# Expert stage of a two-block model: all-token expert chunks spread singly among the row experts, mean sums inside the output projection, one register load ahead of the first routed weight load

## The reference, cut to what matters

```python
h = layer_norm_2(DEEPNORM_ALPHA * h + mixer(h), ...)   # y_out, layer_norm(2l)
y = hier_moe(h, ...)                                   # router, order, experts
h = layer_norm_2(DEEPNORM_ALPHA * h + y, ...)          # layer_norm(2l + 1)

def hier_moe(x, ...):        # 4 groups of 4 experts, hidden width 512
    g_idx = top-1 group of each token; e_w = softmax over its top-2 experts * g_w
    h = silu(x @ w_gate) * (x @ w_up) * gate_of_the_expert
    return h @ w_down
```

## Time and profile before

| | |
|---|---|
| median of three runs | 2466.53 us |
| the profiled execution | 2459.22 us, its span 2457.3 us |
| PE / DVE / ACT busy over the span | 92% / 62% / 43% |
| mean granted TensorE clock | 0.952 of 2.4 GHz |
| expert stage, layer 0: first chunk's matmul to the end of the last scatter | 1459.7 to 1831.6 us |
| expert stage, layer 1 | 2070.5 to 2436.6 us |
| of these, from gate of row expert 4 on | 233.8 and 230.6 us |
| weights read in such a stretch | 324 and 320 GB/s |

### The profile page before, as it was taken

How to read it: one execution, slowest core, us unless ns; L and a number is a source line. 1 busy time by engine, 2 the same in 40 slices (tenths; PEclk the granted TensorE clock), 3 DMA queues, 4 the chain that set the end, 5 groups by cost and what they waited for, 6 DMA issues and landing times.

```text
span 2457.3 us, 36662 instructions
## 1 busy us (share of the span) xinstructions
PE 2271.4 (92%) x13900; PEld 1894.5 (77%) x13900; DVE 1512.9 (62%) x2349; ACT 1068.1 (43%) x1514; POOL 234.8 (10%) x225
## 2 busy tenths in 40 slices
PE   7999999999999999899999679999989786999997
PEld 6677567999767756799976469987778476998875
DVE  3846365755384636575534565589985166658997
ACT  1142433343114244234433234467764264447775
POOL 1814000101181400011000000000000000000000
PEclk9999889999999989999999689999999998999999
DMA  4332113455333212356533125589964412458995
GB/s 164 124 118 79 52 61 129 163 181 173 119 125 124 70 52 69 131 176 195 185 125 107 43 80 170 192 294 349 346 248 165 144 44 102 157 197 318 353 348 188
DMA packets 109807, 396.86 MB, mean 161 GB/s; under 512 B 12088, under 2 KB 14144, under 8 KB 109376
## 3 DMA queue, kind: packets, MB, share of 16 engines
q1 hardware_dynamic: 108576, 393.45, 46.2%
q10 hardware_dynamic: 1056, 1.06, 0.2%
HBM read 393.40 MB, written 1.06 MB: 161 GB/s over the span
## 4 chain that ended last, share of the span: by engine, by line
PE 68%; DVE 18%; ACT 6%; DMA 5%; issue 2%; SPq 0%; DVEq 0%; ACTq 0%
PE psum L524 66%; DVE W_LO L1526 6%; DMA ring<-in_weights 4%; ACT W_HI L1157 2%; DVE region L1531 2%; PE psum L532 1%; DVE region L1534 1%; DVE RS L1563 1%; ACT region L1162 1%; DMA SQ<-in_weights 1%; DVE region L1538 1%; DVE SQ L1531 1%; ACT L1166 1%; ACT SQ L1162 1%; ACT L1162 0%
## 5 line engine op out<-in xcount | busy, mean ns | idle before, releaser
L1526 DVE TENSOR_TENSOR W_LO<-ring,W_HI 128x1024 fp32r<-128x1024 f32 x434 | 531.7, 1225 | 228.6 <-ACT W_HI L1157 220.2
L1157 ACT ACTIVATE W_HI<-ring 128x1024 fp32r<-128x1024 f32 x434 | 460.8, 1062 | 360.3 <-PE psum L524 219.2
L524 PE MATMUL psum<-HN,ring 128*128 128x272 f32 (+1 forms) x1600 | 382.4, 400 | 16.0 <-DVE HN L1538 16.0
L524 PEld LDWEIGHTS psum<-HN,ring 128*128 128x128 f32 x1600 | 309.6, 195 | 84.2 <-issue 24.9
L524 PE MATMUL psum<-X_HI,W_HI 128*128 128x256 f32 x800 | 228.6, 286 | 27.5 <-DVE W_LO L1526 25.8
L524 PE MATMUL psum<-X_LO,W_HI 128*128 128x256 f32 x800 | 225.7, 282 | 0.0
L524 PE MATMUL psum<-X_HI,W_LO 128*128 128x256 f32 x800 | 225.3, 282 | 0.0
L1166 ACT ACTIVATE region<-psum 128x272 f32<-128x272 f32 (+9 forms) x227 | 89.5, 394 | 285.4 <-PE psum L524 266.0
L1526 DVE TENSOR_TENSOR W_LO<-SQ,W_HI 128x1024 fp32r<-128x1024 f32 x128 | 156.8, 1225 | 40.9 <-ACT W_HI L1157 37.4
L524 PEld LDWEIGHTS psum<-X_HI,W_HI 128*128 128x128 f32 x800 | 154.3, 193 | 30.2 <-issue 23.9
L524 PE MATMUL psum<-FN_HI,W_HI 128*128 128x272 f32 (+1 forms) x592 | 168.5, 285 | 0.0
(11 more groups left out here) (281 smaller groups left out, 4283.2 us busy)
## 6 DMA issues: line engine op xcount, KB each, us to landing
ring<-in_weights SPq DMA_DIRECT2D x615, 512.0 KB, 4.2
SQ<-in_weights SPq DMA_DIRECT2D x128, 512.0 KB, 5.2
XT<-in_x SPq DMA_DIRECT2D x1, 1088.0 KB, 5.2
CST<-in_consts SPq DMA_DIRECT2D x1, 1082.5 KB, 7.4
SQ<-bias_by_distance ACTq DMA_DIRECT2D x1, 1024.0 KB, 5.5
out<-XT SPq DMA_DIRECT2D x8, 128.0 KB, 1.9
PAR<-in_params SPq DMA_DIRECT2D x1, 572.0 KB, 8.3
bias_by_distance<-MIX ACTq DMA_DIRECT2D x1, 12.0 KB
```

The lines of the kernel that those rows point to most:

```text
L524: ins = nc.tensor.matmul(dst, w, x, start=start, stop=stop, skip_group_check=True)
L1157: lane(nc.scalar.activation(W_HI[:, s % SPLIT, :], ring_slot(n), ACT.Copy), split_hi)
L1526: lane(nc.vector.tensor_tensor(W_LO[:, s % SPLIT, :], ring_slot(n), W_HI[:, s % SPLIT, :].bitcast(F32), ALU.subtract), split_lo)
```

## The change

1. **y_out and layer_norm.** Behind each of the projections 2 to 7 of `y_out` PE makes one of the eight ones-matmuls of `ln_mean` (`mean_part`); only the last two stay in `layer_norm`.
2. **order.** On PE the iota comes first, then eight transposes, the counts (two matmuls of eight columns in place of five of four), then the other eight. DVE copies the sixteen counts at once, adds two of them before the order is found, and makes two small operations more after ORD is written.
3. **Lead.** ACT and DVE split one or two chunks more before the routing arithmetic (`expert_weights`); the two halves of hidden tile 0 are put apart by a chunk.
4. **Experts.** Wide and row work are now single-chunk steps. After the lead (gate 0, up 0, gate 1) come gate and up of row expert 4, then up 1. The other 16 gate and up chunks of wide experts 2 and 3 are dealt out over row experts 5 to 11, two or three to an expert, and the 16 down chunks over row experts 12 to 15 (the last two behind the last row down). Hidden tile 1 stands behind up 1 and ahead of the turn of expert 4; hidden tiles 2 and 3 behind the turns of experts 8 and 11. Scatters stand behind the turns of experts 13 and 14 and at the end. The rounded outputs of a group go to its slot of XG; hidden tiles 1 to 3 get tiles of their own.
5. **SP.** Only the register of the group that comes next is loaded; the others when their first chunk comes.

The core of the diff:

```diff
+            def mean_part(r, k):
+                if k == 0:
+                    take("ln_mean", r)
+                dst, done = banks.tile(("ln_mean", r)), banks.filled(("ln_mean", r))
+                banks.await_read(pe, ("moe", r // 2, "total", k // 2) if r % 2 else ("y_out", r // 2, k))
+                mm(dst[:, :256], ones(128, 128), ht(k), k == 0, k == KT - 1, done if k == KT - 1 else None)
...
+                pe.wait_ge(sem("before"), l + 1)
                 dst, done = take("iota", l, bank=3)
                 mm(dst[:, :128], ones(128, 128), BEF[:, :], done=done)
+                token_rows(l, 0)
+                pe.wait_ge(sem("group_chosen"), l + 1)
+                dst, done = take("counts", l, bank=2)
+                mm(dst[:, 0:8], ones(128, 128), MS[:, 32:40])
+                mm(dst[:, 8:16], BEF[:, :], MS[:, 32:40], done=done)
+                token_rows(l, 1)
...
+            def abreast(l, *step):          # DVE; ACT has the same
+                follow.to(min(splits.marks["step", step[0], l, *step[1:]][0] + SPLIT - 1, splits.first["moe", l, "last"] + 1))
...
-                for i in range(2):
-                    follow.to(first("gate", 0) + 2 + i)
-                    x_tok_low(l, i)
+                follow.to(first("gate", 0) + 3)
+                x_tok_low(l, 0)
+                follow.to(first("gate", 0) + 4)
+                x_tok_low(l, 1)
+                follow.to(first("gate", 0) + 5)
                 expert_weights(l)
...
+            def hidden(l, e, q):            # DVE
+                abreast(l, "hidden", e, q)
+                wide_hidden(l, e, q)
...
+            def rows_turn(l, e):            # DVE
+                abreast(l, "rows_turn", e)
+                ...
+            def rows_down(l, e, c):         # DVE
+                if (e % GROUP, c) == (GROUP - 1, 3):
+                    abreast(l, "rows_down", e, c)
+                    ...
...
-                    for s in range(4):
-                        group_at[l, s] = sp.value_load(ORD[0:1, s : s + 1], min_val=0, max_val=3 * GROUP_ROWS)
+                if (l, g) not in group_at:
+                    group_at[l, g] = sp.value_load(ORD[0:1, g : g + 1], min_val=0, max_val=3 * GROUP_ROWS)
...
+def experts_order(l):
+    s = [("moe_lead", l)] + row("gate", GROUP) + row("up", GROUP) + wide("up", 1) + hidden(1) + [("rows_turn", l, GROUP)]
+    for e in range(GROUP + 1, NEXP):
+        s += row("gate", e)
+        if e < 3 * GROUP:
+            n = e - GROUP - 1
+            between = (wide("gate", 2) + wide("up", 2) + wide("gate", 3) + wide("up", 3))[(16 * n) // 7 : (16 * n + 16) // 7]
+        else:
+            n = 4 * (e - 3 * GROUP)
+            between = (down(0) + down(1) + down(2) + down(3))[n - n // 8 : n + 4 - (n + 4) // 8]
+        s += between[:1] + row("up", e)[:2] + between[1:2] + row("up", e)[2:]
+        s += row("down", e - 1)[:1] + between[2:3] + row("down", e - 1)[1:] + between[3:]
+        s += [("rows_turn", l, e)]
+        for u in (2, 3):
+            if ("wide", l, "up", u, 3) in between:
+                s += hidden(u)
+        if e > 3 * GROUP and e < 3 * GROUP + 3:
+            s += [("scatter", l, e - 3 * GROUP - 1)]
+    return s + row("down", NEXP - 1) + down(3)[2:] + [("scatter", l, 2), ("moe_done", l)]
```

More of the change, by code:

```diff
@@ L929, in expert_chunks, with expert_chunk, again @@
+            def expert_chunk(l, part, e, c):
+                splits.first["moe", l, part, e, c] = splits.first["moe", l, "last"] = len(splits.chunks)
                 at = EXPERT_CHUNKS * (e % GROUP) + 4 * ("gate", "up", "down").index(part)
-                for c in range(4):
-                    yield c, chunk(True, (l, e // GROUP, at + c))
+                return chunk(True, (l, e // GROUP, at + c))
+            def again(*key):
+                return banks.tile(key), banks.filled(key)
             def gates_turn(l):
@@ L968, in slots_turn @@
                            i == 0, i == 1, done if (s, i) == (2, 1) else None)
[L970 to L992, removed]
-                s = e // GROUP - 1
[L995 to L1000, removed]
+            def wide(l, part, e, c):
+                bank = {"gate": 0 if e < 2 else 4, "up": 6 if e else 2}[part]
+                outs = [again("moe", l, part, e, q) if c else take("moe", l, part, e, q, bank=bank + q) for q in range(2)]
+                w = expert_chunk(l, part, e, c)
+                for k in range(2):
+                    if (part, e) == ("gate", 0):
+                        pe.wait_ge(sem("x_split"), KT * (3 * l + 2) + 2 * c + k + 1)
+                    for j in range(4):
+                        dst, done = outs[j // 2]
+                        last = c == 3 and k == 1
+                        mm(dst[:, 256 * (j % 2) : 256 * (j % 2) + 256], columns(w, 512 * k + 128 * j, 128), x_parts(2 * c + k),
+                           c + k == 0 and j % 2 == 0, last, done if last and j % 2 else None)
@@ new lines, in rows @@
+            def rows(l, part, e, c):
+                s = e // GROUP - 1
+                key = ("moe", l, part, e)
+                dst, done = again(*key) if c else take(*key, bank=(0, 2)[part == "up"])
+                w = expert_chunk(l, part, e, c)
+                for k in range(2):
+                    at = slice(128 * s, 128 * s + 128)
+                    last = c == 3 and k == 1
+                    mm(dst[:, :], (XG_HI[:, 2 * c + k, at], XG_LO[:, 2 * c + k, at]), columns(w, 512 * k, 512), c + k == 0, last, done if last else None)
@@ L1455, in moe, with gate_out, wide @@
-                follow.to(first("down", NEXP - 1) + 4)
-                rows_out(l, 2)
+                gate_out(l, 1)
+            def gate_out(l, e):
+                for q in range(2):
+                    act.wait_ge(sem("hidden"), 2 * (GROUP * l + e - 1) + q + 1)
+                    evacuate(("moe", l, "gate", e, q), SGM[:, 2 * q : 2 * q + 2, :], 512, ACT.Silu)
+            def wide(l, part, e, c):
+                if (part, c) == ("gate", 3):
+                    abreast(l, "wide", part, e, c)
+                    gate_out(l, e)
```

231 lines of the change are left out of this document (116 added, 115 removed).

## The result

The changed kernel takes 2476.4 us (median of 20 runs, 2466.33 to 2486.0); the kernel before, run beside it, 2471.77 us (20 runs, 2463.03 to 2479.16). The ratio is 1.0022, with an interval of 1.0011 to 1.0032: 3 to 8 us slower, well inside the 0.5% that I had called no change. The forecast was 2475.0, reckoned from a median of 2466.53 over three runs of the kernel before; over 20 runs this median is 5.2 us higher.

A forecast was written before the change was run, and what follows sets the result against it. PE's stream, 68% of the chain of waits, was taken to set the end. Halts 4.9, clock 6.8, switching 1.0, registers -3.35, counts -1.1, means 0.6, lead -0.3 sum to +8.5 on 2466.5: 2475.0 us, 8-in-10 range 2450 to 2488.

The forecast's parts named there:

- the mechanism and its places: Expert stage: DVE work between two splits halts PE: 2.9, 6.0, 4.5 us behind turns 4, 8, 11; 2.6 at end.
- The first rival: Expert stage: halts do not gather because splits run further ahead; 5.5 us a layer, no falls, 2447 us; chance 0.23.
- a third more time per chunk: Expert stage: DVE and DMA have a third more time per chunk than in the row stretch; argument for The first rival.
- halts: Expert stage: PE halts of 16.0 us a layer in place of 15.1 and 12.0, so +0.9 and +4.0 us.
- The clock: Expert stage: one fall to 1.2 GHz, 1.7 us, behind each of two long halts a layer, +6.8 us.
- The last rival: Expert stage: longer half-clock stretches behind halts, three more falls a layer, +10.2 us, so 2485 us; chance 0.12.
- the clock stays up: Expert stage: the halts come but without clock falls, +1.7 us in all, 2468 us; chance 0.20.
- Switching: Expert stage: PE changes between 512 and 256 columns some 28 times a layer more, 0.5 us a layer, +1.0 us.
- Registers: Ahead of the first routed load: three register loads go from SP while other engines wait, -3.35 us over two layers.
- Counts: In the order step: DVE's idle before it copies the counts goes, -1.1 us.
- Means: Output projection: moving mean matmuls into it gains nothing and loses 0.28 us a layer, +0.6 us.
- lead: Lead before the experts: gates_turn comes 0.1 us later in layer 0 and 0.4 earlier in layer 1, -0.3 us.

The follow-up runs named there:

- x1: Changed kernel with the DVE work of hidden tiles 1 to 3 in single pieces among the splits; 2444.39 us, ratio 0.9903 to the kernel before.
- x6: Changed kernel with hidden tile 2 whole but moved from behind turn 8 to behind expert 9's row gate; 2466.67 us, ratio 1.0013 to the kernel before.
- x2: Changed kernel plus 22 unused 512-column matmuls on PE before expert 9's fourth gate chunk; 2467.52 us, ratio 1.0000 to the kernel before.
- x4: Changed kernel with the sixteen mean matmuls put back behind the output projection; 2473.45 us, ratio 1.0024 to the kernel before.
- x7_all: Changed kernel, hidden tiles in pieces, means put back, gates_turn one chunk earlier in the lead, a wide chunk before row down 15; 2435.42 us, ratio 0.9890.
- x3: Kernel before with only the register part: one register loaded ahead of the first routed load, others when needed; 2465.87 us, ratio 0.9990.

## Why the prediction was right, and which of its terms were too small

- **Right, the mechanism and its places.** Against an unbroken stream, halts of 2.8, 5.7, 4.3 and 2.0 us stand behind turns 4, 8, 11 and at the end in layer 0 (2.8, 5.7, 4.4, 2.0 in layer 1), where the text has 2.9, 6.0, 4.5 and 2.6. There is no other but one of 1.03 near the stretch's start. Take the burst apart and they go (x1), move it and they move (x6). The first rival, that they would not gather, falls. Its "a third more time per chunk" is also misread: by the text's own terms it is 22.3 / 14 against 16.9 / 12 us, 13% more.
- **Mis-sized, the halts of before.** I had 15.1 and 12.0 us as the rest of a sum. Idle by idle the trace has 10.2 and 9.0 there, and 11.2 and 10.0 over the whole stretch, where the changed kernel has 15.7 and 15.9. The rest of the sum was a fall of the clock (1.6 us in layer 0) and PE's own work with waits too short to count, which I had too short. So the term "halts" is +4.5 and +5.9 us and not +0.9 and +4.0.
- **The clock: right in kind, mis-sized by nearly as much.** Matmul by matmul, against the same shapes at full clock, the falls cost 6.1 us in the stretch of layer 0 and 7.8 in that of layer 1, and 1.6 and nothing in the profiled execution of before. That is +12.3 us where the text has +6.8. It had one fall of 1.7 us behind two bursts a layer. There is one behind each of the three bursts, turn 4's too, and in layer 1 those behind turns 4 and 11 cost some 3 us each. The last rival had this mechanism, with 17.0 us for it; the measured sum lies between the two. The rival "the clock stays up" falls by x2.
- **What the pages state of it.** The Trainium skill (TensorE: Matmul & The Clock Gate, "HAM oscillation") states that waits between bursts of matmuls let PE's clock fall to half. Behind the long halts the traces agree (0.58 behind 5.55 us), and behind 2.37 us they do so in one execution and not in another. Of the two places where the prediction says that the trace agrees, only one does: 0.76 behind 2.91 us, but 1.00 behind 2.39.
- **Switching: no cost is seen.** The text has 0.5 us a layer. At full clock a 512-column matmul is followed by one of 256 columns after 231 ns and by its own kind after 229 (medians of layer 0), and 256 columns are followed by either after 113 or 114. From the changed kernel:

```profile
1643.55 0.39 PE L534 MATMUL psum<-W_HI,XG_LO 128*128 128x512 f32 x1
1643.78 0.28 PE L534 MATMUL psum<-X_HI,W_HI 128*128 128x256 f32 x1
1643.90 0.28 PE L534 MATMUL psum<-X_LO,W_HI 128*128 128x256 f32 x1
```

  With halts and falls taken off, the stretch is 309.3 and 309.0 us before, 308.4 in both layers of the changed kernel, 310.3 and 309.7 in x1_apart. So the term is -1.5 us and not +1.0. The spread of this rest is partly that the wide matmuls' distance takes two values, 113 and 118 ns, at the same clock; why, no run tells. Up 1's 96 wide matmuls take 10.96 us in the changed kernel and 11.36 in x1_apart, in this order:

```profile
1515.80:1526.76 10.96, 10.96 (x98) 10.92 (x98) 7.17 (x7) 4.50 (x5) 0.00 (x0) 1.00 0.93 331
```

```profile
1512.80:1524.16 11.36, 11.36 (x98) 11.32 (x98) 7.25 (x8) 4.49 (x5) 0.00 (x0) 1.00 0.90 319
```

- **Registers** gave -3.6 us, predicted -3.35. **Counts** gave -1.06, predicted -1.1. **Means** by x4 cost 0.8 for both layers, predicted 0.6. The **lead** gave -1.4, predicted -0.3; in layer 0 it is 2.2 us shorter and in layer 1 0.8 longer, which is inside what it varies by between executions (x7_all). The wait before `gates_turn`, for which the text has 4 to 5 us, is 2.2 us in layer 0 and absent in layer 1.
- **Why the total agrees: in part by luck.** By the pair of traces the whole is +17.5 us and the touched parts are +15.8, by the medians the whole is +4.6, and I had +8.5. My terms with the sizes measured give 10.4 + 12.3 - 1.5 - 3.6 - 1.1 + 0.8 - 1.4 = +15.9. So for the pair two terms were too small by 5.5 us each. The medians came out lower than the pair, and that hides it. The interval of the ratio is +3 to +8 us, and +8.5 stands just outside it; that 2475.0 is so near to 2476.4 owes something to the median of three runs that it starts from.
- **Why the medians differ less than the pair** is only partly shown. What I missed is that the kernel before pays for falls too: I took the one execution shown, with a single fall, for the kernel. In x3 the same stage lasts 6.6 us more in its two stretches than in the profiled execution of before, though that is again one execution, 3.6 us above its own median. The mean granted clock is 0.952 in the profiled execution of before and 0.949 in the median of the 29 executions of this kernel beside x1 to x4; among these 29 an execution is 1.3 us longer for each 0.001 less (a straight fit, correlation -0.67). By that fit, an estimate, 4 us of the 12.6 are its clock. Another 1.8 us of the pair's difference lies in code that the change does not touch. The rest stays open; only more profiled executions of the kernel before would tell.

## What to carry to other kernels

When two regimes are interleaved on one engine, look at what the helper engine's queue holds at the seams. Shares of busy time said that there was slack; the halts came from eight operations in one piece between two splits. With the same work in pieces of two to five operations the changed kernel went from 0.2% slower to 1% faster. And a sum of changes against one profiled execution inherits that execution's luck: 12.6 us of it here, more than the effect to be told.

## What the runs showed of the hardware

- The same idle of 2.37 us, at the same place of the same instructions, was followed by a granted clock of 1.00 in one execution and of 0.57 in another.
- 22 matmuls run in idle time, 5.16 us, kept the clock at 1.00 through a wait of 5.55 us and gave back 2.65 us in layer 0 and 1.75 in layer 1.
- Among 29 executions of the kernel before, one with a mean granted clock lower by 0.001 was 1.3 us longer (a straight fit, correlation -0.67).
- At full clock, changing between matmuls of 512 and 256 columns showed no cost: 231 ns from a 512-column matmul to a 256-column one, 229 to one of its own kind.
- With the same operands and the same granted clock, wide matmuls follow each other at 113 or at 118 ns, through whole chunks; the cause is open.
